# Recurrence stage of a decoder layer: joint turning of T, and GpSimd's input chain one tile further ahead

## The chip, the cores and the metric

The kernel runs on one core of a Trainium2 chip. The metric is the device time of one execution in microseconds (us); lower is better. Three runs of the kernel before took 3564.42, 3570.32 and 3578.72 us, median 3570.32. Engines are called as in the profile: PE is TensorE (PEld its weight loads), DVE is VectorE, ACT is ScalarE, POOL is GpSimd, SP is SyncE, which issues the transfers here.

## The reference, cut to what matters

One layer on 2048 tokens of width 1024 in float32: a projection, differential attention and an RWKV-7 time mixing side by side, an output projection, a mixture of experts and a gated embedding. The change is in the time mixing, which has 8 heads of size 64:

```
r, k, v = z + (token_shift(z) - z) * mu_rkv            # three parts of 512 columns
kk = k * k_k;  kk = kk * rsqrt(max(sum(kk * kk), 1e-24))
k  = k * (1 + (a - 1) * k_a)
S  <- S diag(w) + (S a') b'^T + v k^T;   y = S r          # a' = -kk, b' = kk * a, token by token
y  = groupnorm(y) * gn_w + gn_b + sum(r * k * r_k) * v;   out = y * g
```

The kernel does this in chunks of 64 tokens. Inside a chunk the token by token rule becomes a triangular system per head, whose inverse T (64 x 64) is built from blocks of 1, 2, 4, ... 32.

## The kernel before

`phase_rwkv` (from L1023) goes over 16 tiles of 128 tokens, so two chunks a tile; heads of even number are half "a", of odd number half "b". Each engine has a program of its own. All go through 18 steps, -1 to 16. Step i prepares tile i+1 ("prep"), builds T for tile i ("main") and carries the state over tile i-1 and finishes its output ("tail"). Steps -1 and 0 stand alone, steps 1 to 14 are a hardware loop whose body is two steps (a pass), 15 and 16 stand alone again.

What orders the work is written out by hand. Every engine has one semaphore that it raises at each event, in the order of the lists PE_JOBS, ACT_EV, DVE_EV and POOL_EV (from L1006); who needs an event waits for its count. Each engine works through its queue in order, so an instruction that waits holds all behind it. A TensorE job fills one PSUM bank; six banks go round for the main jobs and two for the prep jobs, and a job first waits until the bank's former content was copied out.

The names that the steps below use:

- TensorE: cum (L1515) sums decays; G3, G1, G2 (L1528, L1534) are the products of the four transposed factors cT, of which G3 is the first block level of T. For level l from 1 to 5: Tr(l-1) turns T by a product with the identity (L1538), X(l) multiplies by it (L1542), TX(l) by the turned T (L1546). Level 5 of TX and the last turning, Tr5, are whole jobs for eight heads (L1600, L1602); all others are two, a and b. W, MN, RT, Y0, S0, S1, Y belong to the tail; D and pc and the four T jobs T0 to T3 (L1584, four 128x128 transposes each) to the next tile. The T jobs read Ah, Bh, Rh, Kh.
- ScalarE copies turnings, X, W, D, T jobs from PSUM to SBUF (L1258) and computes P, Pex (L1290, which needs GpSimd's ex), sqk (the squares of kk0) and sqy.
- VectorE fills T from PSUM by a masked copy (L1360), masks G1 and G2 (L1364), makes kp and ssk (L1381 to L1388), evacuates MN (L1392), makes kkn (L1396, needs GpSimd's rsk), the state (L1404, L1408), y and its mean (s1), yc (L1429), Ah (L1431), Bh (L1432), s2, bon and yn (L1437, which needs GpSimd's rsy). kkn, yc, Ah, Bh and yn read both of their inputs from SBUF; the fillings, masks and MN read PSUM.
- GpSimd: the input chain, which is three products on 1536 columns that make rkv of z and the shifted z (L1182, L1184, L1177) and kk0 on 512 columns; then rsk, ex, b, Kh, Rh, rk, T_init (T set to the identity, L1212); then for the tail rsy (after two small products, L1215, L1217), and yo, bv and the output product.
- SyncE (L1098 to L1130): in a step it stores the output of the tile before when GpSimd's output product is done, and then loads z, rkv, sig and a for the tile two ahead.

In the kernel before, TensorE's order of a step is this line (L1590) and those after it:

```
tr(0, "a"); tr(0, "b"); w_("a"); x_(1, "a"); x_(1, "b"); w_("b"); tx(1, "a"); tx(1, "b")
```

Of the kernel before, what the change touches and what calls it, by code (L numbers as in the profile page):

```python
# [10 lines left out]
ALU = mybir.AluOpType  # L11
# [3 lines left out]
P = 128  # L15
SEQ, D = 2048, 1024
TILES = SEQ // P
# [966 lines left out]
class Events:  # L984
# [14 lines left out]
    def in_order(self, name):  # L999
# [6 lines left out]
PE_JOBS = (["cum", "G3a", "G3b", "G1a", "G1b", "Tr0a", "Tr0b", "Wa", "X1a", "X1b", "Wb", "TX1a", "TX1b", "G2a", "G2b",  # L1006
# [3 lines left out]
PREP_JOBS = ("cum", "pc", "T0", "T1", "T2", "T3")  # L1010
TAIL = ("Wa", "Wb", "MN0", "MN1", "RT0", "RT1", "Y0", "S0", "S1", "Ya", "Yb", "sqy", "s1", "yc", "s2", "yn", "ysum", "rsy", "out")
PREP = PREP_JOBS + ("P", "cumsb", "Pex", "sqk", "vcopy", "kp", "ssk", "kkn", "Ah", "Bh", "bon", "T_init", "rkv", "kk0", "rsk", "ex", "b", "Kh", "Rh", "rk", "bv")
ACT_EV = ["P", "cumsb", "Tr0a", "Tr0b", "Wa", "X1a", "X1b", "Wb", "sqk", "Tr1a", "Tr1b", "Pex", "X2a", "X2b", "Y0", "Tr2a", "Tr2b",
          "X3a", "X3b", "Tr3a", "Tr3b", "D", "sqy", "pc", "X4a", "X4b", "vcopy", "Tr4a", "T0", "Tr4b", "T1", "X5a", "T2", "X5b", "T3", "Tr5"]
DVE_EV = ["G3a", "G3b", "G1a", "G1b", "TX1a", "TX1b", "G2a", "G2b", "kp", "ssk", "MN0", "MN1", "kkn", "RT0", "RT1", "TX2a", "TX2b", "S0",
          "S1", "TX3a", "TX3b", "Ya", "Yb", "s1", "yc", "Ah", "Bh", "s2", "TX4a", "TX4b", "bon", "yn", "TX5"]
POOL_EV = ["rkv", "kk0", "rsk", "ex", "b", "Kh", "Rh", "rk", "T_init", "rsy", "bv", "out"]
MAIN_JOBS = [n for n in PE_JOBS if n not in PREP_JOBS]
BANKS = 6
CHUNKS = (slice(0, CK), slice(CK, 2 * CK))  # L1020


def phase_rwkv(nc, t, ident):  # L1023
# [5 lines left out]
    with ExitStack() as ctx:  # L1029
# [3 lines left out]
        assert len(MAIN_JOBS) % BANKS == 0  # L1033
# [13 lines left out]
        TT = two("c_TT", [P, HV, CK]); X = sb("c_X", [P, HV, CK])  # L1047
# [12 lines left out]
        DV = Events(sem("C_dve"), DVE_EV); PO = Events(sem("C_pool"), POOL_EV)  # L1060
        block = ctx.enter_context(nc.Block())

        def bank(name):

            return ps[:, MAIN_JOBS.index(name) % BANKS, :] if name in MAIN_JOBS else ps[:, BANKS + PREP_JOBS.index(name) % 2, :]
# [70 lines left out]
        def _(pool):  # L1136
# [27 lines left out]

            def step(i, s, what, j):
# [13 lines left out]
                if real:  # L1179

                    pool.wait_ge(z_in[n], nth(i + 1, j, 1) * 64 + 64)
                    pool.tensor_tensor(rkv[n][:], rkv[n][:], z[n][:], ALU.subtract)  # L1182
                    pool.drain()
                    pool.tensor_tensor(rkv[n][:], rkv[n][:], mu[:], ALU.mult)  # L1184
                    pool.drain()
                ev("rkv", mul(rkv[n][:], rkv[n][:], z[n][:], ALU.add))
                pool.drain()
                ev("kk0", mul(kk0[:], rkv[n][:, RW:2 * RW], k_k[:]))
# [47 lines left out]
            steps(pool, step)  # L1236

        @block.scalar
        def _(act):
            act.wait_ge(cs_p, 1)  # L1240

            def step(i, s, what, j):
# [23 lines left out]
                def tr(level, f):  # L1266
                    evac(f"Tr{level}{f}", TT[s][:, half(f), :], narrow)
# [4 lines left out]
                def x_(level, f):  # L1272
                    evac(f"X{level}{f}", X[:, half(f), :], narrow)
# [7 lines left out]
                tr(0, "a")  # L1281
                tr(0, "b")
                w_("a")
                x_(1, "a")
                x_(1, "b")
                w_("b")
                ev("sqk", lambda: nc.scalar.activation(sq[:], kk0[:], ACT.Square), (PO, "kk0"))
                tr(1, "a")
                tr(1, "b")
                ev("Pex", lambda: nc.scalar.activation(Pex[:], cumsb[:], ACT.Exp, scale=-DECAY), (PO, "ex"))  # L1290
                x_(2, "a")
                x_(2, "b")
                evac("Y0", Y0[:])
                tr(2, "a")
                tr(2, "b")
                x_(3, "a")
                x_(3, "b")
                tr(3, "a")
                tr(3, "b")
# [4 lines left out]
                x_(4, "a")  # L1304
                x_(4, "b")
                ev("vcopy", lambda: nc.scalar.copy(V[n][:], rkv[n][:, 2 * RW:3 * RW]), (PO, "rkv"), (PE, "Y0"))
# [3 lines left out]
                tr(4, "a")  # L1310
                t_(0)
                tr(4, "b")
                t_(1)
                x_(5, "a")
                t_(2)
                x_(5, "b")
                t_(3)
# [4 lines left out]
        def _(dve):  # L1322
# [16 lines left out]
            def step(i, s, what, j):  # L1339
# [36 lines left out]
                for f in AB:  # L1376
                    masked(f"G2{f}", AR2, f)
                if "prep" in what:
                    dve.wait_ge(PO.sem, PO.value("kk0", i))
# [8 lines left out]
                ev("ssk", lambda: nc.vector.tensor_scalar(ssk[:], ssk[:], 1e-24, None, ALU.max))  # L1388
                for c in range(2):
# [20 lines left out]
                fill_T("TX2a", 2, "a")  # L1410
                fill_T("TX2b", 2, "b")
                state(0)
                state(1)
                fill_T("TX3a", 3, "a")
                fill_T("TX3b", 3, "b")
                if "tail" in what:
                    dve.wait_ge(PO.sem, PO.value("out", i - 1))
                for f in AB:
                    ev(f"Y{f}", lambda: nc.vector.tensor_tensor(heads(y[:])[:, half(f), :], bank(f"Y{f}")[:, 0:4 * DH].rearrange("p (h n) -> p h n", h=4),
                                                                heads(Y0[:])[:, half(f), :], ALU.add), (PE, f"Y{f}"), (AC, "Y0"))  # L1420
                dve.drain()

                def mean():
# [10 lines left out]
                fill_T("TX4a", 4, "a")  # L1434
                fill_T("TX4b", 4, "b")
                ev("bon", lambda: nc.vector.tensor_reduce(bon[:], heads(rk[:]), AX.X, ALU.add), (PO, "rk"))
                ev("yn", lambda: nc.vector.tensor_tensor(heads(y[:]), heads(y[:]), rsy[:].unsqueeze(2).broadcast_to([P, HV, DH]), ALU.mult), (PO, "rsy"))  # L1437
                ev("TX5", lambda: nc.vector.copy_predicated(T[s][:], lv[:, 5, :].unsqueeze(1).broadcast_to([P, HV, CK]),
                                                            bank("TX5").rearrange("p (h n) -> p h n", h=HV)), (PE, "TX5"))

# [3 lines left out]
        def _(pe):  # L1444
            pe.wait_ge(cs_p, 1)

            def step(i, s, what, j):
# [3 lines left out]
                def ready(names, waits):  # L1451

                    asked = list(waits)
                    for name in names:
                        ring, size = (MAIN_JOBS, BANKS) if name in MAIN_JOBS else (PREP_JOBS, 2)
                        k = ring.index(name)
                        e, other = owner(ring[k - size])
                        if k >= size or not first:
                            asked.append((e, other, 0 if k >= size else 1))
# [77 lines left out]
                def tr(level, f):  # L1537
                    chunked(f"Tr{level}{f}", hs_of(f), lambda b, h, r: nc.tensor.matmul(cols(b, h // 2, CK), T[s][r, h, :], i64[r, :], start=True, stop=True),  # L1538
                            (DV, ("G3" if level == 0 else f"TX{level}") + f, 0))
# [1205 lines left out]
```

## Time and profile before

| | us |
|---|---|
| runs, median (lowest to highest) | 3570.32 (3564.42 to 3578.72) |
| the profiled execution | 3570.77 |
| its span, first to last instruction | 3568.9 |
| the recurrence stage in it | about 1264 to 2004 |
| mean granted TensorE clock over the span | 0.943 of full speed |
| TensorE busy, whole span | 3111.6 (87%) |
| VectorE / ScalarE / GpSimd busy, whole span | 2019.4 / 1596.5 / 879.0 |

The span is cut into its stages by the lines that run in it; the recurrence is the stretch in which GpSimd is busy most (6 to 7 tenths in the page's slices) while the transfers are few. A row of the timeline gives the start, the time from the first start to the last end of the merged instructions, engine, line, operation, output and input, shape, count, and in brackets the idle time before it with what ended it. A float32 matmul shows as two records.

### The profile page before, as it was taken

The page shows a single profiled execution, that of the slowest core. Times are in us where ns is not written, and L with a number is a line of the kernel's source. Part 1 is how long each engine was busy: PE and PEld are TensorE (multiplying, and loading weights), DVE is VectorE, ACT ScalarE, POOL GpSimd, SP SyncE. Part 2 cuts the span into 40 slices and gives each one's busy share as a digit, 9 for nine tenths or more (in the row PEclk, how much of TensorE's full clock was granted, in tenths as well). Part 3 has the DMA queues.
Part 4 walks back from the last instruction along what each step waited for, and adds up shares of the span by engine and source line. Part 5 has one row for each costly group of instructions (what it writes and reads, how often), then busy time and mean ns, then how long its engine had stood idle before and what let it go on. Part 6 is the DMA issues. An engine that isn't in the chain of part 4 may idle for free. (4 is left out here: it accounts for less than half of the span.)

```text
span 3568.9 us, 76160 instructions
## 1 busy us (share of the span) xinstructions
PE 3111.6 (87%) x27464; PEld 2515.2 (70%) x27464; DVE 2019.4 (57%) x2950; ACT 1596.5 (45%) x2656; POOL 879.0 (25%) x1064
## 2 busy tenths in 40 slices
PE   7999999988898848888888599569899999996899
PEld 5776878865666637777778488457777777774687
DVE  4333761017777724444444233668788788885555
ACT  3332211007777723333333111057777777775332
POOL 1001320002141366766674100000000000000343
PEclk9999999999999969999999799679999999998899
DMA  5444357444000031211110466536877866773343
GB/s 166 171 171 156 127 179 251 142 132 107 7 16 7 12 125 44 80 63 62 62 62 15 138 215 214 200 110 244 316 284 262 338 258 248 294 264 138 127 147 118
DMA packets 230272, 541.77 MB, mean 152 GB/s; under 512 B 26208, under 2 KB 62176, under 8 KB 221824
## 3 DMA queue, kind: packets, MB, share of 16 engines
q1 hardware_dynamic: 211696, 471.48, 37.5%
q0 software_dynamic: 11552, 41.95, 3.2%
q10 hardware_dynamic: 6768, 24.64, 1.7%
q8 instruction: 194, 3.18, 0.4%
q14 instruction: 62, 0.51, 0.0%
HBM read 408.52 MB, written 129.51 MB: 151 GB/s over the span
## 5 line engine op out<-in xcount | busy, mean ns | idle before, releaser
L559 PE MATMUL p_z<-w_in_part,hn_split 128*128 128x512 f32 x2304 | 538.7, 394 | 8.7 <-DVE w_in_part L388 4.5
L559 PEld LDWEIGHTS p_z<-w_in_part,hn_split 128*128 128x128 f32 x2304 | 435.3, 190 | 100.1 <-DMA hn_split<-s_hT 5.0
L1670 DVE TENSOR_TENSOR e_w_part<-w_gate_up_sb,e_w_part 128x1024 fp32r<-128x1024 f32 x380 | 441.1, 1220 | 105.2 <-ACT e_w_part L1665 105.2
L1665 ACT CAST e_w_part<-w_gate_up_sb 128x1024 fp32r x380 | 372.3, 1046 | 134.0 <-PE pe_y L2420 71.0
L2408 PE MATMUL pe_gate<-e_w_part,e_xT 128*128 128x512 f32 x1128 | 288.6, 414 | 32.8 <-DVE e_w_part L1670 32.8
L2408 PE MATMUL pe_up<-e_w_part,e_xT 128*128 128x512 f32 x1128 | 274.8, 399 | 16.7 <-DVE e_w_part L1670 16.6
L2420 PE MATMUL pe_y<-e_w_part,e_hT 128*128 128x512 f32 x1128 | 277.2, 402 | 7.3 <-DVE e_w_part L1670 7.3
L2408 PEld LDWEIGHTS pe_gate<-e_w_part,e_xT 128*128 128x128 f32 x1128 | 219.1, 198 | 84.7 <-DVE e_w_part L1670 24.4
L2408 PEld LDWEIGHTS pe_up<-e_w_part,e_xT 128*128 128x128 f32 x1128 | 208.8, 188 | 81.2 <-DVE e_w_part L1670 33.1
L2420 PEld LDWEIGHTS pe_y<-e_w_part,e_hT 128*128 128x128 f32 x1128 | 210.4, 190 | 55.1 <-DVE e_w_part L1670 7.7
L1670 DVE TENSOR_TENSOR e_w_part<-w_down_sb,e_w_part 128x1024 fp32r<-128x1024 f32 x188 | 223.5, 1222 | 21.7 <-ACT e_w_part L1665 19.1
L2233 POOL COPY e_idx<-row_tokens 128x1 uint32 (+1 forms) x48 | 10.1, 210 | 859.3 <-PE pe_xT L2385 799.8
L1665 ACT CAST e_w_part<-w_down_sb 128x1024 fp32r x188 | 194.8, 1052 | 50.1 <-PE pe_up L2408 34.3
L1677 PE MATMUL pd_out<-d_w_out_part,d_mixT 128*128 128x512 f32 x768 | 188.2, 401 | 11.9 <-DVE d_w_out_part L1670 11.9
L919 PE MATMUL p_scores<-kT_all,qT_all 64*128 64x512 f32 (+3 forms) x768 | 177.5, 517 | 14.7 <-DVE ident_half L827 14.4
L776 ACT ACTIVATE prob<-p_scores,neg_max 128x640 f32<-128x640 f32 (+5 forms) x240 | 176.6, 743 | 19.4 <-DVE neg_max L848 12.8
L1677 PE MATMUL pf_gate<-f_w_gate,f_hgT 128*128 128x512 f32 x768 | 178.4, 392 | 2.4 <-DVE f_hgT L1670 2.4
L1677 PEld LDWEIGHTS pd_out<-d_w_out_part,d_mixT 128*128 128x128 f32 x768 | 143.7, 190 | 44.1 <-issue 12.3
L415 DVE COPY z_stage<-p_z 128x512 f32<-128x512 f32 x40 | 27.6, 691 | 255.4 <-PE p_z L559 255.4
L1360 DVE COPY_PREDICATED c_T<-c_levels,p_ring 128x256 f32<-128x256 int32 x160 | 68.5, 444 | 182.5 <-PE p_ring L1546 96.6
L1677 PEld LDWEIGHTS pf_gate<-f_w_gate,f_hgT 128*128 128x128 f32 x768 | 145.2, 189 | 33.1 <-DVE f_hgT L1670 2.8
L961 PE MATMUL p_o<-v_all,attnT 128*128 128x128 f32 x1088 | 152.4, 280 | 7.8 <-issue 6.3
(422 smaller groups left out, 5946.9 us busy)
## 6 DMA issues: line engine op xcount, KB each, us to landing
w_gate_up_sb<-in_w_gate_dram SPq DMA_DIRECT2D x32, 2048.0 KB, 15.1
w_gate_up_sb<-in_w_up_dram SPq DMA_DIRECT2D x32, 2048.0 KB, 19.8
w_down_sb<-in_w_down_dram SPq DMA_DIRECT2D x32, 2048.0 KB, 9.8
hn_split<-s_hT SPq DMA_DIRECT2D x48, 1024.0 KB, 5.1
s_y<-e_y ACTq DMA_DIRECT2D x47, 512.0 KB, 7.2
s_hT<-hn_split SPq DMA_DIRECT2D x16, 1024.0 KB, 6.5
s_y<-d_zeros SPq DMA_DIRECT2D x16, 1024.0 KB, 6.6
s_zr<-z_stage SPq DMA_DIRECT2D x48, 256.0 KB, 2.0
```

Source lines behind the costliest of these rows:

```text
L415: nc.vector.tensor_copy(stage[n % Z_STAGES][:], bank).then_inc(ev_dve, 1)
L559: last = nc.tensor.matmul(bank, hs[m % 3][:, a, k, :].bitcast(F32R), w_part(c, b)[:, k, :].bitcast(F32R), start=(k == 0 and a == b == 0), ...
L776: nc.scalar.activation(prob[g % 2][m][:, EDGE[g][c]:EDGE[g][c + 1]], scores_of(n, W[g][c])[:, m, :], ACT.Exp, bias=nmax[g % 2][:, c, m:m + ...
L919: return nc.tensor.matmul(out[:, m, a:b], qT[r, h, ROW[g], :], kT[r, h, k0:k0 + (b - a) // P, :], start=True, stop=stop)
L961: last = nc.tensor.matmul(pO[:], aT[n % 2][:, b * P:(b + 1) * P], v[:, HEAD[g], kb, :], start=(kb == 0), stop=(kb == ROW[g]))
L1360: return nc.vector.copy_predicated(T[s][:, half(f), :], m, src)
L1665: return nc.scalar.copy(high, src)
L1670: return nc.vector.tensor_tensor(low, src, high, ALU.subtract)
L1677: last = nc.tensor.matmul(out, lhsT(a, k), rhs(b, k), start=(start and k == 0 and n == 0), stop=(stop and k == steps - 1 and n == len(PART ...
L2233: pool.tensor_copy(idx[:], ids[:, bass.ds(i, 1)]).then_inc(idx_ready, 1)
L2408: last = nc.tensor.matmul(bank[:], xT[a][:, g % 4 * 2 + k, :], ring[b][:, g % 4, k * DX:(k + 1) * DX], start=first, stop=final)
L2420: last = nc.tensor.matmul(p_y[:, half, :], hT[a][:, g, :], ring[b][:, g, half * BANK:(half + 1) * BANK], start=first, stop=final)
```

## The change

1. Turning of T: Tr0 to Tr4 are one job each now, four transposes of 128 x 128 (two heads' T side by side for both chunks) against the full identity, into a new tile TP. The last turning, Tr5, stays as it was.
2. X(l) has now one job per chunk ("a" is the first 64 tokens of the tile) over all eight heads; TX(l) one job per half as before, but its inputs come from TP and the new layout of X. TX waits for both X jobs and the whole turning; turning and X wait for both halves of the filling before. TX5 is two jobs now.
3. The order of TensorE's jobs within a step and with it the orders of ScalarE and VectorE are new: other jobs stand between X(l) and TX(l) and behind TX(l). VectorE does kp and ssk before the G2 masks and the second filling; ScalarE does Pex after the copies of X2.
4. GpSimd's input chain (rkv, kk0) has a semaphore of its own and is done a tile further ahead: step i computes it for tile i+2, behind T_init and in front of rsy. GpSimd's loop is therefore six passes, and its last steps are written out. The other engines keep their loop of two steps.
5. A job's bank is looked up by a function, since the number of main jobs (44) is no multiple of six.

The diff, cut to its core:

```diff
+PE_JOBS = ["cum", "G3a", "G3b", "G1a", "G1b",
+           "Tr0", "X1a", "X1b", "Wa", "TX1a", "TX1b", "Wb",
+           "Tr1", "X2a", "X2b", "G2a", "G2b", "TX2a", "TX2b", "MN0", "MN1",
+           "Tr2", "X3a", "X3b", "RT0", "RT1", "TX3a", "TX3b", "Y0", "S0",
+           "Tr3", "X4a", "X4b", "S1", "Ya", "Yb", "TX4a", "TX4b", "D", "pc",
+           "Tr4", "X5a", "X5b", "T0", "T1", "TX5a", "TX5b", "T2", "T3", "Tr5"]
...
+ACT_EV = ["P", "cumsb", "Tr0", "X1a", "X1b", "Wa", "sqk", "Wb", "Tr1", "X2a", "X2b", "Pex", "Tr2", "X3a", "X3b", "Y0",
+          "Tr3", "X4a", "X4b", "D", "sqy", "pc", "vcopy", "Tr4", "X5a", "X5b", "T0", "T1", "T2", "T3", "Tr5"]
+DVE_EV = ["G3a", "G3b", "G1a", "G1b", "TX1a", "TX1b", "kp", "ssk", "G2a", "G2b", "TX2a", "TX2b", "MN0", "MN1", "kkn", "RT0", "RT1", "TX3a", "TX3b",
+          "S0", "S1", "Ya", "Yb", "TX4a", "TX4b", "s1", "yc", "Ah", "Bh", "s2", "TX5a", "TX5b", "bon", "yn"]
+AHEAD_EV = ["rkv", "kk0"]
+POOL_EV = ["rsk", "ex", "b", "Kh", "Rh", "rk", "T_init", "rsy", "bv", "out"]
...
+            def ahead(i, s, j):
+                pool.wait_ge(z_in[s], ((i + 2) // 2 if isinstance(i, int) else j + 2 - s) * 64 + 64)
+                pool.tensor_tensor(rkv[s][:], rkv[s][:], z[s][:], ALU.subtract)
+                pool.drain()
+                pool.tensor_tensor(rkv[s][:], rkv[s][:], mu[:], ALU.mult)
+                pool.drain()
+                AHEAD.in_order("rkv")
+                pool.tensor_tensor(rkv[s][:], rkv[s][:], z[s][:], ALU.add).then_inc(AHEAD.sem, 1)
+                pool.drain()
+                AHEAD.in_order("kk0")
+                pool.tensor_tensor(kk0[:], rkv[s][:, RW:2 * RW], k_k[:], ALU.mult).then_inc(AHEAD.sem, 1)
...
                 ev("T_init", lambda: pool.tensor_copy(T[n][:], i64[:].unsqueeze(1).broadcast_to([P, HV, CK])))
+                if not isinstance(i, int) or i < TILES - 2:
+                    ahead(i, s, j)
                 if "tail" in what:
                     pool.wait_ge(DV.sem, DV.value("s2", i))
...
+                def tr(level):
+                    def make(b):
+                        for p in range(4):
+                            last = nc.tensor.transpose(b[:, p * P:(p + 1) * P], T[s][:, 2 * p:2 * p + 2, :].rearrange("p h n -> p (h n)"), ident[:])
+                        return last
+                    job(f"Tr{level}", make, (DV, "G3b" if level == 0 else f"TX{level}b", 0))
...
+                def x_(level, f):
+                    r = CHUNKS[AB.index(f)]
+                    each(f"X{level}{f}", range(HV), lambda b, h: nc.tensor.matmul(cols(b[at(h)], h // 2, CK), AR1[s][r, h, 0, :], T[s][r, h, :], start=True, stop=True),
+                         (DV, "G1b" if level == 1 else f"TX{level - 1}b", 0))
...
+                def tx(level, f):
+                    def make(b):
+                        for h in hs_of(f):
+                            for c, r in enumerate(CHUNKS):
+                                last = nc.tensor.matmul(cols(b[r], h // 2, CK), TP[at(h), h // 2, c, :], X[at(h), c, h // 2, :], start=True, stop=True)
+                        return last
+                    job(f"TX{level}{f}", make, (AC, f"X{level}b", 0), (AC, f"Tr{level - 1}", 0))
...
+                def level(l):
+                    tr(l - 1); x_(l, "a"); x_(l, "b")
+                def filled(l):
+                    tx(l, "a"); tx(l, "b")
+                level(1); w_("a"); filled(1); w_("b")
+                level(2); g12("G2", 3); filled(2); two_jobs(("MN0", "MN1"), mn, (AC, "Wb", 0))
+                level(3); two_jobs(("RT0", "RT1"), rt); filled(3); each("Y0", range(HV), y0); s_(0)
+                level(4); s_(1); two_jobs(("Ya", "Yb"), y_, (DV, "RT1", 0), (DV, "S0", 0)); filled(4)
+                chunked("D", range(HV), d_, (DV, "G2b", 0), (AC, "vcopy", 1)); job("pc", chunk_ends)
+                level(5); t_(0); t_(1); filled(5); t_(2); t_(3)
+                chunked("Tr5", range(HV), lambda b, h, r: nc.tensor.matmul(cols(b, h, CK), T[s][r, h, :], i64[r, :], start=True, stop=True), (DV, "TX5b", 0))
```

## Rows read from the trace of the kernel before

**Rows 1.** Busy time per stretch: one pass of TensorE's loop (window, length, engines).

```profile
core 0: us, PE busy (x) PEld busy (x) DVE busy (x) ACT busy (x) POOL busy (x), PEclk, DMA share, GB/s
1511.40:1596.56 85.16, 70.36 (x1908) 63.77 (x1909) 40.65 (x80) 32.51 (x74) 58.36 (x40) 0.96 0.17 62
```

**Rows 2.** TensorE's waits in that pass: us in total, times, longest.

```profile
PE p_ring L1546 <- ACT c_X L1258: 3.4, 4, 1.6
...
PE p_ring L1602 <- DVE c_T L1438: 2.1, 2, 1.0
```

**Rows 3.** GpSimd's timeline, recurrence.

```profile
1380.92 1.27 POOL L1177 TENSOR_TENSOR c_yo<-c_yo,c_g 128x512 f32<-128x512 f32 x1
...
1507.57 3.42 POOL L1182 TENSOR_TENSOR c_rkv<-c_rkv,c_z 128x1536 f32<-128x1536 f32 x1
...
1518.31 1.26 POOL L1177 TENSOR_TENSOR c_kk<-c_rkv,c_kk 128x512 f32<-128x512 f32 x1 [0.16 <-issue]
...
1529.05 1.27 POOL L1177 TENSOR_TENSOR c_b<-c_kkn,c_a 128x512 f32<-128x512 f32 x1 [0.63 <-DVE c_kkn L1396]
...
1535.37 0.61 POOL L1212 COPY c_T<-c_i 128x512 f32<-128x512 f32 x1
1542.52 0.20 POOL L1215 TENSOR_TENSOR c_tiny<-c_s,c_consts 128x8 f32<-128x8 f32 x1 [6.54 <-DVE c_s L1433]
...
1892.20 1.26 POOL L1177 TENSOR_TENSOR c_yo<-c_yo,c_g 128x512 f32<-128x512 f32 x1
...
1934.18 1.26 POOL L1177 TENSOR_TENSOR c_yo<-c_yo,c_g 128x512 f32<-128x512 f32 x1
```

**Rows 4.** TensorE's timeline, steps 0, 5 and 6.

```profile
1316.74 1.98 PE L1546 MATMUL p_ring<-c_X,c_TT 64*64 64x64 f32 x32 [5.49 <-ACT c_X L1258]
...
1511.40 2.05 PE L1515 MATMUL p_ring<-c_sig,c_maskG 128*128 128x512 f32 x2 [3.34 <-issue]
...
1542.82 1.15 PE L1546 MATMUL p_ring<-c_X,c_TT 64*64 64x64 f32 x32 [0.19 <-ACT c_X L1258]
...
1544.85 0.33 PE L1584 MATMUL p_ring<-ident,c_AD 128*128 128x128 f32 x1
...
1545.44 0.68 PE L1538 MATMUL p_ring<-c_i,c_T 64*64 64x64 f32 x16
...
1558.26 0.97 PE L1542 MATMUL p_ring<-c_T,c_AR 64*64 64x64 f32 x25 [1.10 <-issue]
...
1564.02 0.68 PE L1538 MATMUL p_ring<-c_i,c_T 64*64 64x64 f32 x16 [1.58 <-DVE c_AR L1364]
...
1567.19 0.27 PE L1542 MATMUL p_ring<-c_T,c_AR 64*64 64x64 f32 x1
```

**Rows 5.** The G3 jobs of one step: durations (min/median/max, ns), first and last start.

```profile
L1528 PE MATMUL p_ring<-c_cT x32: 218/218/267, 1553.4 to 1554.2; 64*64 64x64 f32 x32
```

**Rows 6.** Timeline of GpSimd and VectorE in step -1.

```profile
1286.04 1.26 POOL L1177 TENSOR_TENSOR c_cum<-c_cum,c_sig 128x512 f32<-128x512 f32 x1
1286.11 1.75 DVE L1396 TENSOR_TENSOR c_kkn<-c_kk,c_rsk 128x512 f32<-128x512 f32 x1 [1.79 <-POOL c_rsk L1177]
...
1289.09 0.69 DVE L1431 SCALAR_TENSOR_TENSOR c_AD<-c_kkn,c_Pex 128x512 f32<-128x512 f32 x1 [1.24 <-ACTq L1253]
1289.15 1.75 POOL L1177 TENSOR_TENSOR c_Kh<-c_kp,c_invP 128x512 f32<-128x512 f32 x1
...
1289.70 1.75 DVE L1432 TENSOR_TENSOR c_Bh<-c_b,c_invP 128x512 f32<-128x512 f32 x1
```

**Rows 7.** SyncE's last load of a step, and that load's median from issue to landing.

```profile
1511.12 0.64 SPq L1103 DMA_DIRECT2D c_a<-s_lora  x1
...
c_a<-s_lora SPq DMA_DIRECT2D x11, 256.0 KB, 7.3
```

**Rows 8.** VectorE's timeline, steps 5 and 6.

```profile
1514.66 0.94 DVE L1360 COPY_PREDICATED c_T<-c_levels,p_ring 128x256 f32<-128x256 int32 x2 [7.89 <-PE p_ring L1528]
...
1539.41 0.68 DVE L1431 SCALAR_TENSOR_TENSOR c_AD<-c_kkn,c_Pex 128x512 f32<-128x512 f32 x1
...
1554.23 0.78 DVE L1360 COPY_PREDICATED c_T<-c_levels,p_ring 128x256 f32<-128x256 int32 x2 [3.12 <-PE p_ring L1528]
```

More of the change, by code:

```diff
@@ L1005 @@
 AB = "ab"
-PE_JOBS = (["cum", "G3a", "G3b", "G1a", "G1b", "Tr0a", "Tr0b", "Wa", "X1a", "X1b", "Wb", "TX1a", "TX1b", "G2a", "G2b",
[3 rows of a table removed]
+PE_JOBS = ["cum", "G3a", "G3b", "G1a", "G1b",
[5 rows of a table added]
 PREP_JOBS = ("cum", "pc", "T0", "T1", "T2", "T3")
 TAIL = ("Wa", "Wb", "MN0", "MN1", "RT0", "RT1", "Y0", "S0", "S1", "Ya", "Yb", "sqy", "s1", "yc", "s2", "yn", "ysum", "rsy", "out")
[L1012 to L1017, printed above, removed]
+PREP = PREP_JOBS + ("P", "cumsb", "Pex", "sqk", "vcopy", "kp", "ssk", "kkn", "Ah", "Bh", "bon", "T_init", "rsk", "ex", "b", "Kh", "Rh", "rk", "bv")
+ACT_EV = ["P", "cumsb", "Tr0", "X1a", "X1b", "Wa", "sqk", "Wb", "Tr1", "X2a", "X2b", "Pex", "Tr2", "X3a", "X3b", "Y0",
[4 more added lines that the diff above has]
+POOL_EV = ["rsk", "ex", "b", "Kh", "Rh", "rk", "T_init", "rsy", "bv", "out"]
 MAIN_JOBS = [n for n in PE_JOBS if n not in PREP_JOBS]
@@ L1020, with bank_of, before_in_bank @@
 CHUNKS = (slice(0, CK), slice(CK, 2 * CK))
+def bank_of(name):
+    return MAIN_JOBS.index(name) % BANKS if name in MAIN_JOBS else BANKS + PREP_JOBS.index(name) % 2
+def before_in_bank(name):
+    k = PE_JOBS.index(name)
+    for back, names in ((0, PE_JOBS[:k]), (1, PE_JOBS[k:])):
+        same = [other for other in names if bank_of(other) == bank_of(name)]
+        if same:
+            return same[-1], back
 def phase_rwkv(nc, t, ident):
@@ L1234, in step @@
                 ev("out", mul(yo[:], yo[:], g[n][:]))
-            steps(pool, step)
+            ahead(-2, 0, None)
+            step(-1, 1, {"prep"}, None)
+            step(0, 0, {"main", "prep"}, None)
+            with pool.Fori(0, (TILES - 2) // 2 - 1) as j:
+                step(j * 2 + 1, 1, {"main", "tail", "prep"}, j)
+                step(j * 2 + 2, 0, {"main", "tail", "prep"}, j)
+            step(TILES - 3, 1, {"main", "tail", "prep"}, None)
+            step(TILES - 2, 0, {"main", "tail", "prep"}, None)
+            step(TILES - 1, 1, {"main", "tail"}, None)
+            step(TILES, 0, {"tail"}, None)
         @block.scalar
@@ L1272, in x_ @@
                 def x_(level, f):
-                    evac(f"X{level}{f}", X[:, half(f), :], narrow)
+                    evac(f"X{level}{f}", X[:, AB.index(f), :, :], narrow)
                 if "prep" in what:
@@ L1388, in step @@
                 ev("ssk", lambda: nc.vector.tensor_scalar(ssk[:], ssk[:], 1e-24, None, ALU.max))
+                for f in AB:
+                    masked(f"G2{f}", AR2, f)
+                for f in AB:
+                    fill_T(f"TX2{f}", 2, f)
                 for c in range(2):
@@ L1420, in step @@
                                                                 heads(Y0[:])[:, half(f), :], ALU.add), (PE, f"Y{f}"), (AC, "Y0"))
+                for f in AB:
+                    fill_T(f"TX4{f}", 4, f)
                 dve.drain()
@@ L1454, in ready @@
                     for name in names:
[L1455 to L1459, printed above, removed]
+                        last, back = before_in_bank(name)
+                        if not (back and first):
+                            asked.append((*owner(last), back))
                     for e in (AC, DV, PO):
```

90 lines of the change are left out of this document (24 added, 66 removed), and 3 rows, old and new, of the table PE_JOBS.

## The prediction

> **What bounds the kernel now.** The change touches one stage, the recurrence, and everything else stays as it is. I read the busy time of a stretch first: in one pass of TensorE's loop (two steps, 85.16 us) TensorE is busy 70.36 us, GpSimd 58.36, VectorE 40.65, ScalarE 32.51 [rows 1]. So TensorE is the stage's bound, but it stands for 14.8 us of the pass. The waits of TensorE [rows 2] and its timeline [rows 4] say why: 3.4 us for ScalarE's copies of X, which stood in its queue behind Pex and so behind GpSimd; 2.1 us for the last filling of T; 3.34 us at the loop's jump; 1.10 and 1.58 us in front of an X and a turning job of the pass's second step [rows 4]. GpSimd's timeline [rows 3] gives the period: the output product ends step 1 at 1380.92 and step 13 at 1892.20, so 511.3 us for 12 steps, 42.6 a step, 85.2 a pair. The same rows show the chain that is moved: three products on 1536 columns and kk0 run from 1507.57 to 1519.57, 12.0 us, at the head of GpSimd's step.
>
> **The sum is made on the profiled execution** (3570.77 us, span 3568.9), 0.45 us above the runs' median of 3570.32, so a difference carries over as it is. The runs spread from 3564.42 to 3578.72; 0.5% (18 us) is what I take a measurement to tell from no change.
>
> **Part 1: joint turning, coarser jobs.** A turning of T is now four 128x128 transposes. A T job of today is the same four: from 1544.85 to the next job at 1545.44, 0.59 us [rows 4]. The turning it replaces is two jobs of 16 records; 32 such records start over 0.93 us (1.15 less the 0.22 that the last one lasts, the TX job at 1542.82 [rows 4]). Gain 0.34 x 5 = 1.7 us a step. X and TX now keep their rows for a whole job and alternate columns, as G3 does; its 32 records start within 0.8 us [rows 5], against 0.93. Bounds 0 and 0.13 us for each of ten pairs of jobs; I take 0.1, 1.0 us a step, because G3 has just this form. Against that, TX waits for both copies of X and the next level for both fillings; G2, MN, RT, Y, S1, D and the T jobs are now laid between, 0.8 to 2.9 us each time, which is longer than a copy or a filling (0.45 us). So the waits of rows 2 (3.4 and 2.1 us a pair) go. If no more came in their place, TensorE's step would be 4.5 to 5 us shorter.
>
> **Part 2: GpSimd's order.** Per step GpSimd does the same work, in the order rsk, ex, b, Kh, Rh, rk, T_init, *input chain of the tile after next*, rsy, output. What the move buys: kp and ssk no longer wait for kk0, and Pex is ready in time. What it costs has two places. First, rsy now stands behind the 12.0 us, VectorE's yn waits for rsy, and the next step's first filling stands behind yn in VectorE's queue. Second, VectorE's yc, Ah and Bh fall into the chain, and the first T job on TensorE waits for Bh, with T1, TX5, T2, T3 and Tr5 queued behind it, then the next step's cum and G3.
>
> The loads: z_in for the tile after next is asked for in the same step. SyncE issues the four loads behind the output product of the step before, the last of them 3.6 us after it (1511.12 against 1507.57), and it lands 7.3 us later [rows 3, 7]. The output product ends at about 5 us of a step (yn and then five products of 1.0 to 1.3 us), so the landing is at 16; the chain begins at 21.4. SyncE's order is untouched. Nothing is lost there.
>
> **The lock between VectorE and GpSimd.** In step -1 [rows 6] kkn, which has both inputs in SBUF, takes 1.75 us beside GpSimd's ex of 1.26 and ends 0.56 after it; alone such an operation takes 0.68 [rows 8]. Then Ah (0.69) runs and Kh, issued 0.06 us after it, takes 1.75 instead of 1.27; Bh, issued before Ah has ended, takes 1.75 and ends 0.55 after Kh. So they take turns: a VectorE operation with two SBUF inputs waits for the end of the GpSimd operation that it meets, and a waiting GpSimd operation goes ahead of VectorE's next. Operations that read PSUM (fillings, masks) show no such wait. Today yc, Ah and Bh run while GpSimd is idle. In the change they meet the three products of 3.43 us [rows 3]: yc waits for the first, Ah for the second, Bh for the third. Bounds for the three together: 0 (GpSimd and VectorE share freely) and 3 x 3.43; I take the taking of turns, since Ah, Kh, Bh show exactly the pattern.
>
> The trace shows waits of about 0.6 to 1.2 us only, behind products of 1.26 us. The Trainium skill (SBUF — State Buffer, Who interferes with whom) says that the pair of ports is locked for the whole instruction, and that an operation with two SBUF inputs contends with one that reads SBUF. By it the wait grows with the product to 3.4 us, and the sum is the forecast's; if the wait stayed at the measured size, the sum would be the first rival's plus some 2 us a step. No row has a long product beside such an operation.
>
> **A step of the change, in us after VectorE's first filling (G3).** To the end of MN: today 1554.23 to 1567.19, 12.96, of which 2.7 are the two stalls [rows 4, 8]. The new order is G3, G1, Tr0, X1 (waits for the G1 masks as W did, at 2.5), Wa, TX1, Wb, Tr1, X2, G2, TX2, MN: 3.35, 4.2, 5.0, 5.9, 6.7, 7.55, 8.5, 9.25 and with MN's 2.6 to 2.9, 12.0. Then, counted from MN's end M: four evacuations, 1.35, kkn to 2.05 (rsk is done long before, so no wait in it); GpSimd's b to T_init, 6.93 us as from 1529.05 to 1535.98 [rows 3], plus about 0.4 where the state's products hold it, to 9.4; the input chain from there. TensorE: Tr2, X3, RT, TX3, Y0, S0 to 5.65, Tr3, X4, S1 at 7.65, Y and TX4 to 9.6, D, pc, Tr4, X5 to 13.1. VectorE: S1 to 9.8, Y to 10.5, filling to 11.45, s1 to 12.4; yc at 13.2 to 13.75, after it Ah to 17.75 and Bh to 21.75. T0 starts at 21.9: TensorE has stood for 8.8 us.
>
> After a wait of 5.49 us the records show the lower clock: TX2 takes 1.98 instead of 1.15 [rows 4]; the jump's cum takes 2.05 us. I charge 2.5 us for T0, T1 and TX5 at half speed; bounds 0 and 4.5 (all of T0 to Tr5). So T0 and T1 to 24.8, TX5 26.4, T2, T3 and Tr5 to 28.6. rsy is then long done; yn ends at 28.6. Next G3 filling 1.9 us after Tr5: 30.5. Behind the jump it is 3.34 + 3.26 instead (the idle time in front of cum, and from cum at 1511.40 to the filling at 1514.66 [rows 4, 8]): 35.2. A pair is 12.8 + 0.4 (half-clock masks and the MN stall behind the jump) + 30.5, and 12.0 + 1.3 (half of the two stalls, since TensorE's queue can fill while it stands) + 35.2, together 92.2 against 85.2. Steps 1 to 13 hold six such pairs: +42 us.
>
> The ends: step 0 fills an idle GpSimd and has no output to wait for, so that the waits of part 1 go and one lock wait comes: about 4 less (bounds 0 and 6); step 14 has no input chain, so no lock and rsy in time: 13.3 + 21.1 = 34.4 against 42.0 [rows 3], 7.6 less; step 15 has part 1 alone, 3 less. Together -14.6. Sum 42 - 14.6 = +27.4: 3598 us.
>
> **Rivals.** *No turns taken* (0.20). Bh would be ready at M + 14.3, and rsy would bound: chain to M + 21.4, kk0 and rsy with its two small products (2.3 us, from 1542.52 [rows 3]) and yn, end at M + 24.6 to 27. Pairs of 80.7, six times -4.5, -27, and -14.6: 3529. For it: no row with long products; against it: rows 6. *Two of the three pass together* (0.10): one product less in each step, 3.4 us, pairs of 85.3; only the ends are left, 3556. *The clock stays low* (0.08): the wait in front of T0 is longer than that of 5.49 us [rows 4], and each step has 8.8 us of standing; with 4.5 us instead of 2.5 in each step and the whole 2.7 of stalls kept, 5.4 us a pair more, +32 on the forecast: 3630. It decides from the point where the low clock outlasts TX5. The side other than mine is the first: it decides where GpSimd's waiting product does not go ahead of Ah, and then the next bound is rsy at 39 us a step.
>
> **How the numbers follow.** The forecast has 0.62. Its own range is 3556 (no clock charge, no stalls: 85.3 a pair, ends kept) to 3635. The whole range, 3525 to 3638, takes in the first rival and most of the last. Within the forecast I give slower 0.68, same 0.25, faster 0.07, since its parts can lose 10 us each; the first rival is faster to 0.9, the second same to 0.6 and else faster, the last slower. Together faster 0.26, same 0.24, slower 0.50.
>
> **What would show it.** In the changed profile, each step 1 to 13: Ah and Bh of about 4 us instead of 0.68, right behind the ends of the rkv products, and no wait in kkn (0.69); ScalarE free of Pex's wait; T0 after a wait of 8 to 9 us for Bh; records of T0 and T1 at half speed; pairs near 92 us; step 14 near 34. Wrong: Ah and Bh of 0.7 to 2 us beside products of 3.43, then TensorE waits for T from yn at the head of a step and the kernel is faster. If the turning jobs take over 0.9 us, part 1 is wrong, and if the jump costs nothing beside T0's wait, the pairs are 3 us shorter.

## The result and the profile after

The change makes the kernel slower: 3626.49 us median (3611.18 to 3630.16, 4 runs) against 3572.36 (3564.42 to 3578.72, 4 runs), a ratio of 1.0152 [1.0131, 1.0173]. The prediction was 3598, slower. The direction and the mechanism held, the size did not: 26 us were forecast over the median of 3572 and 54 came. The profiled execution took 3630.16 us, its span 3628.3 (before 3568.9). The rows and the lengths of periods are those of one profiled execution of each kernel.

GpSimd's output product again gives the period. It ends at 1379.98 in step 1 and at 1967.20 in step 13: 587.2 us for the 12 periods against 511.3 [rows 3], a pair of 97.9 us where the prediction had 92.2. The last three periods take 97.7 us against 110.2. From the stage's first product to the end of step 1 there are 2.3 us more than before. So the loss is all in the six pairs: +76, where +42 was forecast.

Busy time of one pass of TensorE's loop, which answers to [rows 1], and of the pass before it (each within 1 us of a whole pass):

```profile
core 0: us, PE busy (x) PEld busy (x) DVE busy (x) ACT busy (x) POOL busy (x), PEclk, DMA share, GB/s
1524.00:1621.90 97.90, 65.06 (x1627) 58.15 (x1627) 53.69 (x82) 30.48 (x64) 60.19 (x41) 0.84 0.16 56
1621.90:1719.50 97.60, 70.24 (x1628) 61.57 (x1628) 53.21 (x82) 30.39 (x64) 59.42 (x40) 0.80 0.16 56
```

The joint turning leaves fewer records (1628 for 1908), yet in the second of these passes TensorE is busy for the same 70 us (in the first for 65), at a granted clock of 0.80 instead of 0.96 of full speed. VectorE is busy 12.6 us more with nearly the same work (82 records for 80). TensorE's waits in the second pass, which answer to [rows 2] (total, times, longest):

```profile
PE p_ring L1613 <- DVE c_Bh L1457: 11.7, 2, 6.8
PE p_ring L1585 <- issue: 4.3, 1, 4.3
PE p_ring L1535 <- issue: 3.5, 1, 3.5
PE p_ring L1574 <- issue: 2.4, 2, 1.9
PE p_ring L1579 <- issue: 1.4, 1, 1.4
PE p_ring L1596 <- issue: 1.1, 1, 1.1
```

The waits for X and for the last filling are nearly gone, as forecast. In their place stand T0's wait for Bh, twice a pass, and a new idle time of 4.3 us in front of the MN job (L1585) that no engine ends. First the wait for Bh. VectorE and GpSimd in the pass's first step, before T0:

```profile
1649.28 2.23 DVE L1433 TENSOR_TENSOR c_S<-c_Stmp,c_pc 128x256 f32<-128x256 f32 x1
...
1653.71 1.13 DVE L1451 TENSOR_SCALAR c_s<-c_s 128x8 f32<-128x8 f32 x1
1654.93 0.69 DVE L1454 TENSOR_TENSOR c_y<-c_y,c_s 128x512 f32<-128x512 f32 x1
1655.54 3.92 DVE L1456 SCALAR_TENSOR_TENSOR c_AD<-c_kkn,c_Pex 128x512 f32<-128x512 f32 x1
1659.38 1.75 DVE L1457 TENSOR_TENSOR c_Bh<-c_b,c_invP 128x512 f32<-128x512 f32 x1
```

```profile
1647.59 3.63 POOL L1184 TENSOR_TENSOR c_rkv<-c_rkv,c_z 128x1536 f32<-128x1536 f32 x1
1651.37 3.44 POOL L1186 TENSOR_TENSOR c_rkv<-c_rkv,c_mu 128x1536 f32<-128x1536 f32 x1
1654.95 3.96 POOL L1189 TENSOR_TENSOR c_rkv<-c_rkv,c_z 128x1536 f32<-128x1536 f32 x1
1659.07 1.51 POOL L1192 TENSOR_TENSOR c_kk<-c_rkv,c_kk 128x512 f32<-128x512 f32 x1 [0.16 <-issue]
```

yc is 0.02 us ahead of the third product, which is then held (3.96 for 3.44). Ah waits for that product's end and takes 3.92 us, Bh waits for kk0 and takes 1.75. The first two products hold two other operations: the state's product with pc (L1433), which takes 0.6 us where it meets none, and the small multiplication of the mean (L1451), which took 0.17 before. They end within 0.3 us of the products' ends (1651.22 and 1654.81). The T jobs in the pass before, behind Bh (the time in brackets is the idle time ahead of the record):

```profile
1612.02 0.45 PE L1613 MATMUL p_ring<-ident,c_AD 128*128 128x128 f32 x1 [7.88 <-DVE c_Bh L1457]
1612.26 0.42 PE L1613 MATMUL p_ring<-ident,c_Rh 128*128 128x128 f32 x1
```

Here one transpose starts 0.21 us after another, so four take 0.86 us, at a granted clock of 0.50 between 1612 and 1615 us; in the T job of [rows 4] four started within 0.59. Now the second place, W and MN of the pass's second step:

```profile
1675.38 1.03 PE L1579 MATMUL p_ring<-c_AD,c_TT 64*64 64x128 f32 x14 [1.40 <-issue]
1683.98 0.37 PE L1585 MATMUL p_ring<-c_WU,c_Bh 64*64 64x64 f32 x1 [4.34 <-issue]
1688.03 0.42 PE L1586 MATMUL p_ring<-c_V,c_Kh 64*64 64x64 f32 x2
1688.37 0.86 PE L1561 MATMUL p_ring<-ident,c_T 128*128 128x128 f32 x4
```

and what SyncE issued just before it:

```profile
1675.01 0.33 SPq L1116 DMA_DIRECT2D c_z<-s_zr  x1
1675.53 0.33 SPq L1117 DMA_DIRECT2D c_rkv<-s_zr  x1
1676.04 0.33 SPq L1118 DMA_DIRECT2D c_sig<-s_lora  x1
1676.56 0.72 SPq L1119 DMA_DIRECT2D c_a<-s_lora  x1
```

The queues of the DMA engines in 1676 to 1680 and in 1680 to 1684 us (packets, MB, share of 16 engines):

```profile
q1 hardware_dynamic: 296, 1.42, 96.2%
```

```profile
q1 hardware_dynamic: 344, 0.78, 51.0%
q8 instruction: 1, 0.02, 1.5%
```

TensorE stands while the loads fill the DMA engines, and the one instruction packet of these 8 us starts at 1681.64 and lands at 1682.61, when the burst is over. The rest of MN then runs at a granted clock of 0.50, to 1688.37: 4.4 us, where the same records take 2.6 in the pass's first step. In the kernel before, no idle time "issue" apart from the jump was longer than 1.9 us in the 12 periods. That suggests that instructions were held up behind the loads; the experiments had to decide.

### The profile page after: what moved, and what is told of

It reads as the page before. It is cut to its first block and busy times, and to the rows that moved or that the text cites. A ratio compares the mean times of both kernels' runs of the same rounds, so it can differ in the third digit from the quotient of the medians.

```text
span 3628.3 us, 71326 instructions
## 1 busy us (share of the span) xinstructions
PE 3080.2 (85%) x25224; PEld 2472.3 (68%) x25224; DVE 2106.6 (58%) x2966; ACT 1579.8 (44%) x2576; POOL 889.1 (25%) x1064
## 5 line engine op out<-in xcount | busy, mean ns | idle before, releaser
L2437 PE MATMUL pe_gate<-e_w_part,e_xT 128*128 128x512 f32 x1128 | 285.5, 410 | 31.9 <-DVE e_w_part L1699 31.9
L2437 PEld LDWEIGHTS pe_up<-e_w_part,e_xT 128*128 128x128 f32 x1128 | 208.7, 188 | 83.8 <-DVE e_w_part L1699 35.5
L1383 DVE COPY_PREDICATED c_T<-c_levels,p_ring 128x256 f32<-128x256 int32 x192 | 77.9, 442 | 186.7 <-PE p_ring L1574 112.8
```

Of the source, the lines that this page charges most:

```text
L1383: return nc.vector.copy_predicated(T[s][:, half(f), :], m, src)
L2437: last = nc.tensor.matmul(bank[:], xT[a][:, g % 4 * 2 + k, :], ring[b][:, g % 4, k * DX:(k + 1) * DX], start=first, stop=final)
```

## Experiments

The theory (A) has two parts: the lock between VectorE and GpSimd makes Bh late, and the loads hold up TensorE's instructions in MN. The rivals: the coarser jobs themselves cost (B), or TensorE's low clock comes of something other than its standing idle (C). Each kernel is compared by its median with the kernel before that ran beside it, and by the length of the 12 periods: 511.3 before, 587.2 after. The median of the kernel before was 3572.36, 3567.28, 3566.68 and 3570.70 us in the four groups of runs, so a difference between two changed kernels is good to some 6 us. The periods of "loads late" and of "early, pieces" come from executions 7 us below and 7 us above the kernel's median, those of the others from executions within 5 us of it.

**The products in pieces.** The kernel after, with each of the three products cut into three of 512 columns.

```diff
-                pool.tensor_tensor(rkv[s][:], rkv[s][:], z[s][:], ALU.subtract)
+                cut = [slice(k * RW, (k + 1) * RW) for k in range(3)]
+                for c in cut:
+                    pool.tensor_tensor(rkv[s][:, c], rkv[s][:, c], z[s][:, c], ALU.subtract)
```

> The changed kernel with the three products on 1536 columns of the input chain cut into nine on 512 columns, same arithmetic. Theory 1 (a VectorE operation with two SBUF inputs waits for the end of the GpSimd operation it meets, however long): Ah takes about 1.2 to 1.9 us instead of 3.9, Bh is ready 3 to 5 us sooner, the wait in front of T0 falls from 6.8 to about 3; pairs 6 to 9 us shorter, about 3580 us (3565 to 3600). Rival (the two share, or the wait has a fixed size not set by the product's length): no change, 3626 us, Ah stays near 3.9.

Measured: 3565.89, ratio 0.9998 [0.9985, 1.0011], 12 periods 524.9, a pair 10.4 us shorter where 6 to 9 were expected. GpSimd has more instructions for the same elements, and the kernel is 60 us faster than the one after. Its groups between 1380 and 1880 us (busy, mean ns), and those of the kernel after:

```profile
L1461 DVE SCALAR_TENSOR_TENSOR c_AD<-c_kkn,c_Pex 128x512 f32<-128x512 f32 x11 | 19.3, 1754 | 0.0
L1462 DVE TENSOR_TENSOR c_Bh<-c_b,c_invP 128x512 f32<-128x512 f32 x11 | 19.2, 1748 | 0.0
```

```profile
L1456 DVE SCALAR_TENSOR_TENSOR c_AD<-c_kkn,c_Pex 128x512 f32<-128x512 f32 x10 | 39.2, 3919 | 0.0
L1457 DVE TENSOR_TENSOR c_Bh<-c_b,c_invP 128x512 f32<-128x512 f32 x10 | 17.4, 1745 | 0.0
L1613 PE MATMUL p_ring<-ident,c_AD 128*128 128x128 f32 x40 | 16.8, 420 | 61.4 <-DVE c_Bh L1457 61.4
```

Ah's length follows the length of the product that it meets, 3.92 or 1.75 us. That is the lock. B falls as the main cause, since the coarse jobs are all still there; the 13.6 us by which the 12 periods stay longer than before leave room for a small part of it. The gain is not the lock's alone: TensorE's stall in MN (24.1 us in 6 times in the kernel after) shrinks here too, and the kernels without loads below tell the two apart.

**Ah and Bh early.** The kernel after, with Ah right behind kkn and Bh behind level 3's filling, ahead of the products.

```diff
+DVE_EV = [..., "kkn", "Ah", "RT0", "RT1", "TX3a", "TX3b",
+          "Bh", "S0", "S1", "Ya", "Yb", "TX4a", "TX4b", "s1", "yc", "s2", "TX5a", "TX5b", "bon", "yn"]
```

> The changed kernel (3626 us) with one difference: VectorE makes Ah right after kkn and Bh right after the filling of level 3, so before GpSimd's input chain begins; yc stays where it was. Theory 1 (turns are taken between VectorE's two-input operations and GpSimd's products, and TensorE waits for Bh): the waits of 6.8 and 4.9 us in front of T0 go, and with them the half-speed records behind them; a pair of steps falls from 97.9 us to about 84 (then rsy and yn bound it), six times -14: about 3542 us, between 3525 and 3565. Theory 2 (instruction supply of TensorE is what makes it slow; it stalls 12.7 us a pass in the changed kernel): only the T0 waits shorten where supply allows, the stalls grow in their place: 3595 us or more.

Measured: 3581.72, ratio 1.0031 [1.0010, 1.0051], 12 periods 542.9. That is 45 us off the kernel after, between the two expectations. T0 waits for Bh no longer, but in its place for pc, and the MN stall stays (1380 to 1880 us):

```profile
PE p_ring L1576 <- issue: 22.7, 10, 3.7
PE p_ring L1615 <- ACT c_pc L1330: 22.5, 6, 4.3
PE p_ring L1537 <- issue: 19.4, 6, 3.7
PE p_ring L1587 <- issue: 18.9, 6, 4.1
```

ScalarE's square (sqy) waits for yc, which is still locked (2.14 us in the mean, up to 3.88), and pc's copy stands behind it in ScalarE's queue.

**No loads.** The kernel after without the loads of z, rkv, sig and a that SyncE issues inside the steps (the load of g and the store stay). The tiles behind compute with old data, so the experts get other tokens and the later stages other lengths (the total is 3658.3); only the 12 periods are compared.

```diff
-                load(i + 2, s)
+                sp.sem_inc(z_in[s], 64)
```

> The changed kernel without the loads of z, rkv, sig and a inside the stage, except for the first two tiles (the semaphore is raised instead, so later tiles use old data; the output is not the reference's). Theory A (the stalls of TensorE marked issue, 4.3 us in MN, 1.4 in W, 1.9 in TX4 per pass, are instruction fetches held up behind these loads): they go, with 1 to 2 us of half-speed work, so 6 to 9 us a pair less, about 3580 us. Theory B (they have nothing to do with the loads, they are where the fetch comes, whatever the transfers): 3626 us, stalls in the same places and of the same size.

Measured: 12 periods 555.3, a pair of 92.55. TensorE's stretch from 1560 to 1595 us has the Bh wait, but only a short stall in MN:

```profile
1563.84 1.03 PE L1579 MATMUL p_ring<-c_AD,c_TT 64*64 64x128 f32 x14 [0.85 <-issue]
1569.43 0.27 PE L1585 MATMUL p_ring<-c_WU,c_Bh 64*64 64x64 f32 x1 [1.33 <-issue]
1594.97 0.45 PE L1613 MATMUL p_ring<-ident,c_AD 128*128 128x128 f32 x1 [5.76 <-DVE c_Bh L1457]
```

The loads cost 31.9 us over six pairs, 5.3 each, where 6 to 9 were expected: 3.0 at MN's stall in the step shown, and about 1.8 by MN's matmuls at full speed again.

**The kernel before, without its loads** (the same edit and the same caution).

> The kernel before with the same loads left out in the same way (its output is not the reference's). Theory A: the stalls of 1.10 and 1.58 us of the second step go, 3 us a pair, about 3554 us. Theory B: 3572 us, stalls as before.

Measured: 12 periods 518.2 against 511.3. The kernel before loses nothing to its loads, so here B's expectation held and A's, 3 us a pair less, did not: stalls of about 1 us are there with and without loads, and only the long ones of the kernel after are the loads' doing. What grew is TensorE's wait for ScalarE's copies of X, from 24.3 to 30.1 us between 1380 and 1880 us; why was not looked into.

**Loads late.** The kernel after, with SyncE waiting for MN1 before it issues the loads.

```diff
+                if not isinstance(i, int) or i > 0:
+                    sp.wait_ge(PE.sem, PE.value("MN1", i))
                 load(i + 2, s)
```

> The changed kernel, in which SyncE issues a step's loads only when TensorE has finished MN (from step 1 on), 8 us or so later. Theory A (instruction fetches are held up behind the loads): the stalls in front of and inside MN (1.4 and 4.3 us a pass) shrink to 1.5 in all, as without loads, but the input chain begins some 2 us late for want of its data, and Bh with it: 3605 to 3620 us. Theory B (place of the fetch alone decides): the MN stall stays at 4.3 us, and the time rises by the late chain to about 3650 us.

Measured: 3601.99, ratio 1.0099 [1.0070, 1.0128], 12 periods 557.9. That is 3 us under A's range, and MN's stall shrank as A said; that TensorE would stand elsewhere was not expected. The long stall left MN and now stands at Y0 (L1598) in every step, where part of it falls into what T0 would have waited (1380 to 1880 us):

```profile
PE p_ring L1598 <- issue: 41.2, 11, 4.4
PE p_ring L1615 <- DVE c_Bh L1459: 28.1, 10, 3.6
PE p_ring L1587 <- issue: 7.8, 6, 1.4
```

The stall moved when nothing but the time of the loads moved. With the kernel after without loads this shows its cause.

This kernel also bears on C. The stage in the kernel after, with late loads, and with the products in pieces:

```profile
1380.00:1966.00 586.00, 413.19 (x9709) 363.35 (x9700) 321.88 (x492) 181.26 (x382) 361.53 (x240) 0.81 0.16 56
1380.00:1966.00 586.00, 451.05 (x10459) 399.33 (x10459) 296.74 (x527) 194.37 (x408) 371.90 (x253) 0.81 0.16 57
1380.00:1966.00 586.00, 454.50 (x11127) 400.50 (x11118) 309.66 (x558) 202.89 (x425) 405.43 (x333) 0.86 0.17 58
```

The first number behind the comma is TensorE's busy time, 0.81 or 0.86 the granted clock. With late loads TensorE stands nearly as little as with the pieces, yet its clock is that of the kernel after. So the sum of the idle time alone does not set the clock, and C is not settled by these runs.

**The two parts alone.** First the chain moved back to a step's head, behind the output product, with all of the joint turning kept:

```diff
-                if not isinstance(i, int) or i < TILES - 2:
-                    ahead(i, s, j)
...
                 ev("out", mul(yo[:], yo[:], g[n][:]))
+                if not isinstance(i, int) or i < TILES - 2:
+                    ahead(i, s, j)
```

> Part 1 alone, nearly: the changed kernel with GpSimd's input chain put back behind its output product, so that it makes rkv and kk0 for the next step's tile as the kernel before does; TensorE's, ScalarE's and VectorE's new orders are kept. Theory 1 (the chain beside yc, Ah and Bh is what costs; the turning and the coarser jobs are gains): no lock wait, T0 does not wait for Bh; kp and ssk wait for kk0 instead, and GpSimd's chain closes a loop of about 42 us a step: pairs of 84 to 87 us, 3550 to 3565 us. Rival (the coarser jobs and barriers of part 1 cost by themselves): waits of TensorE for fillings and X copies, 3600 us or more.

Measured: 3603.82, ratio 1.0100 [1.0072, 1.0128], 12 periods 558.8. That is the rival's time, and TensorE does wait for copies of X, but not because the jobs are coarse. The lock is gone (Ah takes 0.68 us in every step). In its place kp and sqk, which now stand ahead of jobs that TensorE needs, wait for kk0 (1380 to 1880 us):

```profile
ACT c_sq L1315 <- POOL c_kk L1192: 103.0, 11, 11.7
DVE c_kp L1402 <- POOL c_kk L1192: 95.2, 11, 10.9
PE p_ring L1574 <- ACT c_X L1288: 88.0, 22, 10.4
```

Then the kernel before with the chain moved as in the change, and its own order of jobs:

```diff
-POOL_EV = ["rkv", "kk0", "rsk", ...
+AHEAD_EV = ["rkv", "kk0"]
+POOL_EV = ["rsk", ...
```

> Part 2 alone: the kernel before with only GpSimd's input chain moved (a tile further ahead, between T_init and rsy). Theory 1: Ah and Bh take up to 3.9 us here too, and in the old order of VectorE the filling of level 4 and then the one of level 5 (behind yn, which waits for rsy) stand behind them: 4 to 5 us a step more, about 3630 us (3605 to 3655). Rival (only the new orders make the chain harmful): about the time before, 3565 to 3580 us.

Measured: 3654.96, ratio 1.0253 [1.0219, 1.0288], 12 periods 597.6, where TensorE waits for late fillings up to 6.4 us; Ah takes 3.92 us here too. So each part alone is slower than the kernel before, part 1 by 37 us and part 2 by 88, and the two together lie between, at 54: against the kernel before, the new order of jobs saves 34 us once the chain stands where it does, and moving the chain costs 17 us once the new order is there.

**Early, pieces, and the square late.** Both cures, and sqy moved behind T1's copy.

> The changed kernel with three differences: Ah and Bh before the input chain (as in e2_ah_bh_early), the chain's products in pieces of 512 columns (as in e3_pieces), and ScalarE's sqy, which waits for yc, behind the copies of T1 instead of in front of pc, vcopy and the copies of level 5. Theory 1: nothing of TensorE waits behind a locked operation any more; rsy and yn bound the step at 37 to 39 us, pairs of about 80 to 82, 3520 us (3505 to 3545). Rival (TensorE's instruction supply fills the room): stalls marked issue grow beyond 15 us a pass, pairs of 85 or more, 3550 us.

Measured: 3570.58, ratio 1.0008 [0.9985, 1.0031], 12 periods 530.3: a miss. VectorE's yn waits for GpSimd's rsy (DVE c_y L1471 <- POOL c_rsy L1211: 51.0 us in 11 times, up to 7.7), and I took the late square for the cause. The same kernel with sqy left in its place:

> The kernel after with Ah and Bh computed early and the products in pieces, ScalarE's square left in its place before the carried powers. If the late square cost e7_early_pieces_sqy (3570.6) its time through the second normalisation, this one is at 3545 to 3560. Rival: Ah and Bh ahead of VectorE's fillings are themselves the cost, and it stays at 3565 to 3580.

Measured: 3563.13, ratio 0.9977 [0.9961, 0.9992], 12 periods 533.2. Its interval is under 1, and the median lies between the two expectations. The square is not shown to be the cause: the intervals of the two kernels overlap, the periods are no shorter, and yn waits for rsy here too (45.2 us in 11 times, up to 6.5). The MN stall is back in both, here with 17.4 us in 6 times, up to 4.3.

**Pieces and loads late.** The two edits that each helped alone.

> The kernel after with two edits that each gave time alone: the chain's three products in pieces of 512 columns (3565.9 alone, 12 passes 524.9) and the step's loads issued behind MN1 (3602.0 alone, 12 passes 557.9, against 587.2 of the kernel after). If the wait for the product and the stall of TensorE's instruction stream behind the loads are two separate costs, the sum is 587.2 - 62.3 - 29.3 = 495.6 for the 12 passes, about 3537 (3525 to 3550). Rival: with the wait for Bh gone, the late loads fall on S and Y0 with nothing to cover them, and the stall only changes place: 3560 to 3570.

Measured: 3599.50, ratio 1.0080 [1.0064, 1.0096], 12 periods 555.8, outside both expectations. 31 us are lost over the 12 periods against the pieces alone. The largest loss is one line, Y0's stall, with 32.5 us more; the stalls in front of TX fall from 17.8 to 2.0 us, the wait for Bh grows by 4, and the granted clock between 1380 and 1966 us is 0.83 instead of 0.86 (1380 to 1880 us, first this kernel, then the pieces with loads where they were):

```profile
PE p_ring L1620 <- DVE c_Bh L1464: 42.0, 11, 4.9
PE p_ring L1603 <- issue: 41.2, 11, 4.4
```

```profile
PE p_ring L1618 <- DVE c_Bh L1462: 38.0, 10, 4.9
PE p_ring L1579 <- issue: 17.8, 10, 3.7
PE p_ring L1601 <- issue: 8.7, 9, 1.2
PE p_ring L1590 <- issue: 6.3, 6, 1.7
```

**Pieces without loads.** The same caution as for the other kernels without loads.

> The products in pieces, and the stage's loads from step 3 on left out: the later tiles compute with old data, so the stages behind it have other work, and only the stage's 12 passes are compared. The loads alone were worth 31.9 us of the 12 passes (587.2 to 555.3) and the pieces alone 62.3 (to 524.9). If the late loads took back the gain of the pieces in e10_pieces_loads_late (555.8) because the instruction stream is held up wherever the burst lies, this kernel has no such stall: 493 to 500. Rival: the late loads cost something else, and without any loads the passes stay at 520 or above.

Measured (one execution): 12 periods 519.8, 5.1 less than with loads. That is the rival's answer, at its edge: with the products in pieces the loads, issued behind the output product, seldom hold TensorE up (3.75 us in one step and 2.34 in another), and there was little left to cure. Issued behind MN1 they hold it up in each step. The cost of the loads is thus no constant of the kernel but a matter of when they start. The four kernels also split the gain of the pieces: without loads the pieces are worth 35.5 us over the 12 periods (555.3 to 519.8), with loads 62.3; the other 26.8 us are loads that no longer hit a bad moment.

**All three: early, pieces, loads late.**

> All three edits: early Ah and Bh, pieces, loads behind MN1. If the waits for products and for instructions were the whole price, 3520 to 3540. Rival: no better than pieces with late loads alone, as nothing waited for Bh any longer (1.2 us a step left): within 5 us of that kernel or above it.

Measured: 3563.69, ratio 0.9977 [0.9966, 0.9988], 12 periods 521.7, again outside both. It stands 36 us under the pieces with late loads: with Bh out of the way, Y0's stall of up to 4.4 us remains, but no wait for Bh follows it, only shorter ones, for pc up to 1.6 us. This kernel and the one without the late loads are the only two whose interval lies under the kernel before, by 0.2%.

## Why the prediction was off in size

- **The bound and part 1.** The waits for X and for the last filling are gone as stated. At the full clock a turning of four transposes takes 0.63 to 0.66 us, next to the 0.59 forecast from the T job.
- **The lock.** It exists, and scales with the product, as the pieces show. The Trainium skill (SBUF — State Buffer, Who interferes with whom) has the shared ports locked for a whole instruction, and the trace agrees, with 3.92 us beside a product of 3.44. Ah takes 3.9 us in each step. The victims were others than forecast: yc meets a product in one step of twelve (3.74 at 1602.53), and Bh meets only kk0, so it takes 1.75. The first two products hold the state's product (up to 2.79 us) and the mean's multiplication (1.13 to 3.21 us in all steps but one), which the prediction did not list. The end is the same, since it is GpSimd's chain that sets it: T0 starts 22.2 to 22.7 us behind MN's end, where 21.9 was forecast. Its wait is 3.4 to 7.9 us instead of 8.8, since TensorE itself arrives later. T0, T1 and TX5 run at the low clock, as charged, in some steps T2 and T3 too; from T0 to the end of Tr5 it is 5.7 to 7.0 us, 6.3 in the mean, against 6.7 charged.
- **The failed step: "1.3 (half of the two stalls, since TensorE's queue can fill while it stands)".** This half came from no row. In the second step of the pass shown the stalls in W and MN did not halve from 2.7 us but grew to 5.7 (1.40 and 4.34), and MN behind them runs at the low clock for 1.8 us more: 7.5 us where 1.3 was charged. Over all six passes the two stalls are 4.5 us in the mean. From the first filling to MN's end that step takes 17.2 to 19.6 us, 18.1 in the mean, where 13.3 was charged, and from there to the next filling 34.9 where 35.2 was. The pass's first step is 43.7 to 46.8 us against 43.7. I had followed the loads to their landing in front of the chain and found nothing lost, but had not asked what else their burst meets. The kernel without loads has a pair of 92.55 us against the forecast's 92.2, with 13.6 and 35.3 us for the same two parts of the second step: the rest of the sum for a pair holds. Six pairs were 34 us longer than forecast; with 4 us less gained at the ends and 6 us gained outside the stage, where the two kernels are the same, that is the 32 us between the span's difference (59.4) and the forecast's (27.4).
- **The ends.** Forecast -14.6, measured about -10: the last three periods gained 12.5 where 10.6 was forecast (step 14 less than forecast, 40.6 us long for 34.4; the two after it gained more, 4.5 and 6.6 us), while up to the end of step 1 the stage lost 2.3 where 4 was to be gained.
- **The rivals.** No turns taken, and two of three passing together, are refuted by Ah's 3.9 us. The clock that stays low comes nearest in time (3630), and half of it is true: the stalls were kept whole, and more. Its other half is not: T0 to Tr5 are in the mean not slower than charged. With the pieces the granted clock between 1380 and 1966 us rises from 0.81 to 0.86, but with late loads it stays at 0.81, so what sets it is not shown.

Why the burst hits now and did not before can be read from when the loads are issued, counted from the first filling of the step. In the kernel before the load of z goes out 0.1 us or 3.9 to 5.6 us ahead of the filling, step by step in turn. In the kernel after it goes out 0.1 to 2.5 us behind it in a pass's first step and 4.8 to 6.2 us behind it in the second, and there MN stands 3.5 to 4.3 us each time; with the pieces 0.2 to 4.3 us and 7.1 to 9.4 us behind it. In the 12 periods of these three kernels every idle time "issue" over 2.5 us, the jump aside, follows loads that were issued 2.5 to 6.2 us behind the filling. What stays open is why just these times are bad: the trace shows neither which packet a stalled engine waits for, nor when it was asked for.

## What to carry over

Before a long GpSimd instruction is moved, look at which VectorE operations with two SBUF inputs it will lie beside, and who waits for them: each can cost a whole instruction's length, and cutting the long one in pieces takes much of that back without touching the order (62 us of the 12 periods here, 36 of them with no loads in play). And a transfer has more to collide with than its consumer: when a change shifts where a step's loads start, look at TensorE's "issue" idle times beside the DMA share, since a stall of 1.3 us became one of 4.3. A cure that worked alone (late loads, -25 us) can cost more (+34) on a kernel whose waits have moved; it has to be timed in the kernel in which it is to stay.

## What the runs showed of the hardware

- A burst of loads of 2 MB, with 96% of the DMA engines taken, lengthens an idle time of TensorE that no engine ends from 1.3 to 4.3 us, and MN's matmuls behind it, at a granted clock of 0.50, take 4.4 us for 2.6. The Trainium skill (Runtime: NRT & Kernel Launch, Instruction fetch mechanics) has the crossing from one block of instructions to the next as mostly hidden; if that is what TensorE stands for here, it was not hidden once in each pass, and the measurement decides.
- The lock works in both directions: a VectorE operation of 0.68 us that met a product of 3.4 took 3.9, and the product that began 0.02 us behind yc took 3.96 for 3.44. It also holds very small operations: one of 128x8 elements took 1.13 to 3.21 us for 0.17.
